# Two feed-forward layers as 2x2 block products with seven products for eight, in a two-block sequence kernel

## The reference

```python
h = layer_norm(DEEPNORM_ALPHA * h + m @ w_out[l], ln1_g[l], ln1_b[l])
f = jnp.square(jax.nn.relu(h @ w_ff1[l])) @ w_ff2[l]      # 1024 -> 4096 -> 1024
h = layer_norm(DEEPNORM_ALPHA * h + f, ln2_g[l], ln2_b[l])
```

## Time and profile before

| | |
|---|---|
| median of 3 runs | 2612.5 us (2607.85 to 2614.89) |
| span of the profiled execution, first to last instruction | 2605.7 us |
| PE busy | 2510.6 us (96%) |
| DVE, POOL, ACT busy | 1361.5 us (52%), 1034.6 us (40%), 633.4 us (24%) |
| feed-forward part | from about 1854 us to the end |
| DMA | 178.40 MB, mean 68 GB/s |

### The profile page before, as it was taken

The page is one execution under the profiler, slowest core; times in us unless marked ns, Lnnn a source line. Parts: engine busy times, 40 slices in busy tenths (PEclk is TensorE's granted clock), DMA queues, the critical chain, the costliest instruction groups (busy, mean ns, idle before and its releaser), DMA issues.

```text
span 2605.7 us, 34941 instructions
## 1 busy us (share of the span) xinstructions
PE 2510.6 (96%) x13322; PEld 2056.9 (79%) x13322; DVE 1361.5 (52%) x1592; ACT 633.4 (24%) x714; POOL 1034.6 (40%) x467
## 2 busy tenths in 40 slices
PE   7999999999999799999999999999899999999996
PEld 5778888887888588778778787888678888888885
DVE  6765565556511751223366666556845435445357
ACT  4332232222201211350122222221421111111113
POOL 4443433343433643233222332334444444444441
PEclk9999999998999899999999999999899999999998
DMA  5112222122111321122212222221011111111111
GB/s 197 49 58 73 73 80 73 64 89 81 41 48 60 110 89 59 64 101 77 93 62 74 78 69 73 85 97 48 25 49 49 49 48 48 48 48 49 48 49 65
DMA packets 77307, 178.40 MB, mean 68 GB/s; under 512 B 8225, under 2 KB 34081, under 8 KB 76210
## 3 DMA queue, kind: packets, MB, share of 16 engines
q1 hardware_dynamic: 36288, 119.55, 13.8%
q10 hardware_dynamic: 40946, 57.78, 6.5%
HBM read 149.98 MB, written 27.33 MB: 68 GB/s over the span
## 4 chain that ended last, share of the span: by engine, by line
PE 84%; DVE 8%; issue 3%; DMA 2%; ACT 2%; POOL 1%; ACTq 0%; DVEq 0%; POOLq 0%
PE pt L1486 71%; PE pt L1516 2%; PE pt L1502 2%; DMA eb<-o_d 1%; PE wk L1783 1%; DVE eb L1324 1%; PE wk L1641 1%; PE wk L1553 1%; PE wk L1642 1%; PE wk L1753 1%; PE wk L1818 1%; PE wk L1817 1%; PE wk L1541 1%; PE wk L1822 1%; PE wk L1705 0%
## 5 line engine op out<-in xcount | busy, mean ns | idle before, releaser
L351 POOL TENSOR_TENSOR w_hi<-w_raw,ones 128x1024 fp32r<-128x1024 f32 x202 | 390.3, 1932 | 1468.6 <-PE pt L1486 1403.5
L355 POOL TENSOR_TENSOR w_lo<-w_raw,w_hi 128x1024 fp32r<-128x1024 f32 x202 | 588.3, 2912 | 15.8
L1486 PE MATMUL pt<-h,w_hi 128*128 128x512 f32 x1376 | 439.6, 401 | 8.6 <-POOL w_lo L355 4.6
L1486 PE MATMUL pt<-l,w_hi 128*128 128x512 f32 x1376 | 426.2, 391 | 0.0
L1486 PE MATMUL pt<-h,w_lo 128*128 128x512 f32 x1376 | 425.3, 390 | 0.0
L1486 PE MATMUL pt<-xh,w_hi 128*128 128x512 f32 x976 | 305.6, 395 | 7.3 <-POOL w_lo L355 4.8
L1486 PEld LDWEIGHTS pt<-l,w_hi 128*128 128x128 f32 x1376 | 259.3, 188 | 55.7
L1486 PEld LDWEIGHTS pt<-h,w_lo 128*128 128x128 f32 x1376 | 258.9, 188 | 55.5
L1486 PE MATMUL pt<-xh,w_lo 128*128 128x512 f32 x976 | 302.7, 392 | 0.0
L1486 PEld LDWEIGHTS pt<-h,w_hi 128*128 128x128 f32 x1376 | 250.6, 189 | 64.2 <-issue 6.3
L1486 PE MATMUL pt<-xl,w_hi 128*128 128x512 f32 x864 | 269.0, 393 | 0.0
(11 more groups left out here) (355 smaller groups left out, 3314.1 us busy)
## 6 DMA issues: line engine op xcount, KB each, us to landing
w_raw<-ws_d SPq DMA_DIRECT2D x204, 512.0 KB, 3.4
x_raw<-xT_d SPq DMA_DIRECT2D x32, 256.0 KB, 7.4
rowb<-acs_d ACTq DMA_DIRECT2D x8, 1024.0 KB, 4.6
qkc<-qk_d ACTq DMA_DIRECT2D x9, 512.0 KB, 3.9
pp_d<-ebuf ACTq DMA_DIRECT2D x8, 512.0 KB, 3.3
sz_d<-eb ACTq DMA_DIRECT2D x8, 512.0 KB, 2.6
eb<-pp_d ACTq DMA_DIRECT2D x8, 512.0 KB, 4.2
qk_d<-ebuf ACTq DMA_DIRECT2D x8, 512.0 KB, 2.7
```

Source lines behind the costliest of these rows:

```text
L351: nc.gpsimd.tensor_tensor(out=w_hi[:, u, :], in0=w_raw[:, u, :], in1=zeros, op=ALU.add).then_inc(w_hi_done, 1)
L355: nc.gpsimd.tensor_tensor(out=w_lo[:, u, :], in0=w_raw[:, u, :], in1=w_hi[:, u, :].bitcast(f32), op=ALU.subtract).then_inc(w_split, 1)
L1486: ins = MM(pt[:, slot, h * HALF:(h + 1) * HALF], wt[:, w, k * P:(k + 1) * P], x[:, k, h * HALF:(h + 1) * HALF], start=first and k == 0 and ...
```

## The change

Both layers are cut into 2x2 blocks, and each 2x2 block product is made of seven products (Strassen's scheme in the form with shared sums). The two blocks of the contraction and the two blocks of the output channels are those of the weights, and the contraction and the two halves of the tokens are those of the activations. A `product` is one 128x512 result over 4 contraction steps: 4 x 3 = 12 matmuls with one weight operand of 128x512 (`wr_h`, `wr_l`, rings of 4). ACT writes its high part (`weight_hi`) and POOL its rest (`weight_lo`).

First layer: 16 pairs of output tiles x 7 products = 112 products. The seven weight operands are the raw quarters or sums of them (four DVE sums a pair, `pair_sums`; POOL makes them for the first two pairs). The seven activation operands (B11, B21, B22, T1 to T4) are made once, at the layer norm: DVE makes 16 sums (`operand_sum`) and 16 rests (`operand_rest`) of 128x512. For each pair DVE then combines the products (`out_u2`, `out_s5`, `out_22`, `out_12`, `out_21`), squares them and makes the sums that the second layer wants of its activations; SP writes these seven operands to DRAM (`fx_d`, 7 x 256 KB a pair).

Second layer: 4 blocks x 7 stages x 4 products = 112 products. For each stage SP loads one 1 MB operand from `fx_d` (`factor_load`, three buffers), ACT takes its high part (`factor_hi`, two of 128x1024) and DVE the rest (`factor_rest`). The weight sums are made in SBUF (`block_sums`: 16 of 128x512 a block, in stages 0, 1, 2). DVE adds each product straight from PSUM (`add_product`). In the last block the sums for the layer norm are made along with it (`last_sum`, `stats`). The layer-norm output also goes to DRAM (`h_d`) and comes back before the second layer, since its place is used for staging in between. The hardware loops of this part are written out.

```diff
-        def ff1(b):
-            with dve.Fori(0, KT // 2) as j:
...
+        def block_sums(b, q, i):
+            r, done = raw2[b % 2][q], 16 * b
+            if i == 0:
...
+                TT(out=s1b[:, q, :], in0=r[:, 1, 0, :], in1=r[:, 1, 1, :], op=ALU.add).then_inc(s2_done, 1)
...
+                TT(out=s2b[:, q, :], in0=s1b[:, q, :], in1=r[:, 0, 0, :], op=ALU.subtract).then_inc(s2_done, 1)
...
+        for b in range(FF_BLOCKS):
+            final = b == FF_BLOCKS - 1
+            for i in range(7):
+                for q in range(4):
+                    add_product(b, i, q)
+                    if i < 3:
+                        block_sums(b, q, i)
+                    if final and i == 2:
+                        last_sum(q)
+                        stats(q)
+                    if final and i == 4 and q:
+                        stats(3 + q)
...
+                    e, left = divmod(28 * b + 4 * i + q + 4, 4)
+                    if left == 0 and 2 <= e < 7 * FF_BLOCKS:
+                        factor_rest(e)
...
+        def product(out, g, x, first, alone, ready=None, between=None):
+            pe.wait_ge(wl_done, g + 1)
+            for k in range(4):
+                if ready is not None:
+                    pe.wait_ge(ready[0], ready[1] + k + 1)
+                for n, (wt, xx) in enumerate(((wr_h, x[0]), (wr_h, x[1]), (wr_l, x[0]))):
+                    ins = MM(out, wt[:, g % 4, k * P:(k + 1) * P], xx[:, k, :], start=first and k == 0 and n == 0,
+                             stop=k == 3 and n == 2, skip_group_check=not alone)
...
         for h, u in ((0, 0), (0, 1)):
             last_copy(h, u)
             last_square(h, u)
+        for g in range(4):
+            weight_hi(g)
+        last_copy(1, 0)
+        last_square(1, 0)
         ln1(0)
...
+        sp.wait_ge(w_split, S_FF)
+        pair_load(0)
...
+                    pe.wait_ge(xs_lo, XL_BASE + 2 * e + 2)
+                    product(wk[:, q, :] if i == 2 else bank(q), FF1_PRODUCTS + g, xs[e % 3], i in (0, 2, 3, 5), i == 2)
```

More of the change, by code:

```diff
@@ L784, in _ @@
         last_square(1, 1)
-        weight_high(S_FF)
-        for q in range(2, 2 * KT):
+        for q in range(2, 5):
             ln1(q)
-        def ff1(b):
[L790 to L809, removed]
@@ new lines, in _ @@
+        first_product(0)
+        ln1(5)
+        ln1(6)
+        first_product(1)
+        ln1(7)
+        weight_hi(4)
+        act.wait_ge(mm_done, S_FF)
+        ln1(8)
+        ln1(9)
+        relu(0)
+        ln1(10)
+        ln1(11)
+        weight_hi(5)
+        ln1(12)
+        act.wait_ge(stat_done, 7)
+        relu(1)
+        ln1(13)
+        weight_hi(6)
+        ln1(14)
+        operand_hi(0)
+        ln1(15)
+        weight_hi(7)
+        for i in range(1, 8):
+            operand_hi(i)
@@ new lines, in _, with factor_hi @@
+        weight_hi(8)
+        weight_hi(9)
+        for i in range(8, 12):
+            operand_hi(i)
+        weight_hi(10)
+        for i in range(12, 16):
+            operand_hi(i)
+        for g in range(11, 14):
+            weight_hi(g)
+        act.wait_ge(tx_done, 16)
+        act.wait_ge(bl_done, 12)
+        act.wait_ge(h_put, X_BASE + 16 * 2 * KT)
+        square_11(0)
+        square_11(1)
+        for g in range(14, 17):
+            weight_hi(g)
+        def factor_hi(e):
+            act.wait_ge(xs_in[e % 3], X_BASE + 16 * (e // 3 + 1))
+            for m in range(2):
+                A(xs[e % 3][0][:, 2 * m:2 * m + 2, :], xsf[e % 3][:, 2 * m:2 * m + 2, :], ACT.Copy).then_inc(xs_hi, 1)
@@ L1390, in normalise @@
             h, k = divmod(q, KT)
+            if stats == 6:
+                k = (k + 4 * h) % KT
             dve.wait_ge(spread_done, stats + h)
@@ L1466, in _ @@
+        stats(14)
+        stats(15)
+        normalise(4, nrm, 2 * KT, 8)
+        normalise(5, nrm, 2 * KT, 8)
         ln_scale(1, 8)
-        for q in range(4, 2 * KT):
-            normalise(q, nrm2, 2 * KT, 8)
+        for q in range(6, 2 * KT):
+            normalise(q, nrm, 2 * KT, 8)
     @block.tensor
@@ L1871, in in_ff, with in_first @@
+        def in_first(k):
+            if k == 1:
                 ln_sums(1, (a_used, KT))
[L1872 removed]
+            if k == 3:
                 ln_spread(1, 8)
[L1875 to L1884 removed]
```

605 lines of the change are left out of this document (496 added, 109 removed).

## The result

The change made the kernel faster: 2578.05 us median of 4 runs (2576.28 to 2582.50) against 2610.32 for the kernel before on the same chip, a ratio of 0.988 with a 95% interval of 0.9864 to 0.9897. The span of the profiled execution is 2574.6 us, 31.1 under the 2605.7 of before; 17.5 was forecast. The direction and the range held, the size did not: the gain in span was 1.8 times what was predicted.

A forecast was written before the change was run, and what follows sets the result against it. PE was taken to bound the kernel: 87.5 us of matmuls removed, less 2 (waits), 22 (start), 13 (blocks 0 to 2), 29 (block 3) and 4 (clock), gives 17.5 us gained, 2595 us. The range was 2548 to 2632.

The forecast's parts named there:

- the waits between products: On PE, two or three waits a product, over 224 products: 2 us lost, bounds nothing or 4.5.
- the price of POOL's turn: Second layer: each POOL subtraction holds DVE's SBUF-only work for about 1.17 us, 0.1 us of it hidden.
- the clock: PE drops to a lower clock after perhaps eight waits, up to 2.4 us each: 4 us lost, bounds 0 and 19.
- The start: First products around the layer norm, three things late in turn: 22 us lost, bounds 8 and 35.
- The bank wait at product 17: First layer's start: product 17 waits for a bank that comes free 18 DVE and five POOL instructions later, at 1941.9 us.
- The loads: DMA: 8 MB ahead in SP's queue, stage 3's factor lands about 30 us into the block, wanted at some 36: no loss.
- Blocks 0 to 2: Second layer: DVE with POOL's turns makes PE wait before stages 2 and 3: 13 us lost, bounds 0 and 8 a block.
- Block 3: Last block with tail: added layer-norm sums on DVE delay `factor_rest`, so PE waits: 29 us lost, bounds 10 and 45.
- Step (1): At the start: four `weight_hi` ahead of `last_copy(1, 0)` hold ACT, first product at 1860 us where 1854.94 stood.
- PE as the bound in the second layer: Rival, chance 0.25: POOL's subtractions fall beside PSUM adds, nothing is late; gain 63.5 us, 2549 us.
- DVE as the bound in the first layer: Part of rival "DVE is the bound throughout", chance 0.15: POOL subtractions stand in full in DVE's queue; 15 us there, 2624 us.
- The queue of loads late: Rival, chance 0.10: at 250 GB/s the loads ahead of stage 3 make PE wait some 16 us; 2611 us, no change.

The follow-up runs named there:

- the exchange: Changed kernel with ACT's `factor_hi(0)` ahead of the next weight operand: ratio 0.9850, length 720.4 us from first product to end, against the changed kernel's 723.7.
- the run with more turns: Changed kernel with DVE waiting four times in its layer-norm run for POOL's rests of operands 8 to 11: ratio 0.9854, length 714.6 us.
- the small chain: Stand-alone rebuild of DVE sum, ACT rounded copy, DVE remainder, ten times, in no kernel: POOL stood 8.81 and 10.09 us in two of four stretches.
- the small run: Stand-alone run of five stretches of DVE sums beside POOL subtractions, in no kernel: DVE and POOL took turns in all five; POOL's took 1.57 to 1.71 us.

## Why the prediction was wrong in size

The mechanism held: PE is the bound of the first layer, and DVE, slowed by its turns with POOL, keeps PE waiting at the start and in the last block. The sum was 14 us short. The step that failed most is the comparison with before: the waits between products were a loss of 2 us, and before's own losses were left out; together they are a gain of 7.4. The second is the losses of the second layer, 10.5 us too high with the tail, as far as the rows show by the price of POOL's turn. The third is the clock, a separate 4 us that is inside the others. The start and the boundary were 5.5 and 4.4 us worse than forecast and hid part of that.

**Right.** What is removed: 384 matmuls at 0.2267 us are 87.1 (87.5 forecast). The first layer's steady state costs nothing; PE was busy 240.00 of 240. The bank wait at product 17. The exclusive turns of DVE and POOL, with PSUM readers untouched. PE's waits for `factor_rest` in block 3. The loads: the factor for stage 3 landed 33.5 us into block 0 (30 forecast), and PE did not wait for it.

**Before's own losses, +7.4 where -2 stood.** The price of 0.2278 us a matmul had the waits between tiles in it (3.1 us over the 2880), and the forecast carried it over to the 2688 matmuls that are left, which run at 0.2267; its waits of 0.02 us a product weren't there. And before took 4.3 us more than the pitch for its last two tiles. Most of that is the layer norm's sums and the spreading of its scale, 3.5 us of PE's work that the changed kernel has too, in products 217 and 221. The forecast charged 3.5 us for the sums in block 3 as new and set nothing against them. This step is 9 us of the 14 that are missing.

**Blocks 0 to 2, -7.0 for -13.** The step that failed is the price of POOL's turn, 1.17 us. It is 0.8 (1.48 less 0.68), because the subtraction starts inside the PSUM addition. Stage 0 so takes DVE 2.72 us a product, PE's own pace, where 15.5 us for 10.9 had been forecast. What blocks 1 and 2 lose is 0.9 us each. Block 0 loses 5.2, most likely because DVE comes into it late, behind the last pair's `out_` steps and with `factor_rest` of the first stages still to do: it takes up product 112 at 2218.64, 6 us after product 113 has begun. In the run with the first factor ahead, products 116 and 117 go at 3.4 us, DVE's pace. This was only read from the rows.

**Block 3, -24.5 with the tail for -29.** No wait stood before stage 2 (3.1 forecast). Before stage 3 it was 5.5 with the clock (5.6), before stage 4 8.8 (12.6). At the layer norm's sums it was 4.4 (3.5), but only some 0.9 of it is the wait for `stats(7)`, forecast as 2 to 3; the sums themselves are 1.8, and the lower clock behind them 1.7. The spreading at product 221 is 1.7 more. The order of the waits is right; the one that is missing and the one too long fit the lower price of a turn. That the statistics are a part is shown by putting them a stage later (5.1 us back in these products). That DVE's total work sets when stage 4 can begin is shown by the two runs with the remainder first: from 207 to 212 they lost what they had lost without it, within 0.6 us.

**From one layer to the next, -4.4 for 0.** ACT's queue wasn't followed past the end of the first layer: a load that came late held `factor_hi(0)`. Shown by the exchange, which removed it, though 1.9 us came back in block 0.

**The start, -27.5 for -22.** Its end was 4 us off (product 21 at 1958.0, forecast 1954), but that is luck: its steps were off by 1 to 13 us and cancelled. Step (1) failed: the subtraction at 1842.96 in the earlier trace rows is that of the first feed-forward tile, not the last of the projection, so the four `weight_hi` went ahead of time and not behind; the first product came at 1850.87, not 1860, 9.1 us sooner (0.6 of it lie ahead of this part). From there to the last `ln1` the forecast had 30.5 us, as before; it took 41.5. The prediction said that ACT waits inside the layer norm, and priced it at nothing. The longest of these waits:

```profile
1885.17 0.63 ACT L992 ACTIVATE wr_h<-fsum 128x512 fp32r<-128x512 f32 x1 [3.92 <-POOL fsum L568]
...
1886.61 1.49 DVE L1701 TENSOR_TENSOR T1f<-yr 128x512 f32<-128x512 f32 x1 [4.51 <-ACT yr L999]
```

ACT stands behind one of the weight sums that POOL makes for the first two pairs, and DVE behind ACT. That these waits are the 11 us was read from the rows, and no run tests it. Then DVE's run of sums and rests ended 8.5 us sooner than forecast against the last `ln1`, since POOL got one turn in it where seven had been counted, and DVE's `out_` steps 12.8 us later against the end of that run, since they waited for products 8 to 13. POOL shut out by DVE's run is 8 us of that, as the run with more turns shows; no row of before shows it in that form. The last two steps, to product 17 and to product 21, were 3.2 sooner and 1.0 later. The clock of 0.81 over 110 us, charged elsewhere in the forecast, is in all of these.

**The rivals.** PE as the bound in the second layer was nearer than I gave it credit for: true of blocks 1 and 2, false of block 3. DVE as the bound in the first layer didn't occur, and the run with eight more sums shows that it was some 6 us a pair away. The queue of loads late: the factor for stage 3 didn't keep PE waiting in the changed kernel; in versions that came there sooner product 123 lost 1.7 to 2.1 us.

## What to carry to other kernels

When a change takes a known amount from one engine and gives to others, the losses at the seams (the start, the last block) decide its size. Read them product by product against the pitch, in the kernel before too: losses that it already has there are not the change's. Some go along with what is removed, and others, like the layer norm's sums here, stand on both sides and must not be charged as new. The order in which the queues work is worth looking at as well: waits and exchanges on DVE, ACT and SP gave 20.8 us here with no instruction less, where the change itself had gained 31.1. But in a queue that is full, putting one thing first only moves the wait (products 207 to 212), or makes it worse where it passes something that is wanted sooner (product 217). How much room an engine has is shown by giving it work that nobody reads, as the eight sums did.

## What was not expected of the hardware

A POOL subtraction of 1.27 us stood 12.50 us in the kernel, in each of five profiles, and 8.81 and 10.09 us in the small chain, for as long as DVE's SBUF-only instructions followed each other at 0.60 us. In another stretch of the same chain, and in all with independent sums, it got in after one instruction (1.26 to 1.79 us), and DVE's next sum took 1.75. (The Trainium skill, SBUF — State Buffer, "Who interferes with whom", gives the port pair as an exclusive lock, and the turns of 1.75 us agree with it.)

A PSUM-reading DVE addition took 0.68 us whether or not POOL was at work, so an SBUF-only sum behind it is held only for what is left of POOL's turn: 1.48 us in the kernel and 1.15 to 1.37 in the small run, for 1.75 behind another SBUF-only sum.
